# A transformer step with 32 experts on one core: the last expert's rows reach their tokens by one-hot products on TensorE instead of through HBM

## The reference

```python
xn  = rms_norm(h, ffn_norm_g)
g   = argmax(xn @ w_router_group)                  # one of 4 groups
top_v, top_i = top_k(expert logits inside group g, 2)
e_w = softmax(top_v) * softmax(group logits)[g]    # two weights for each token
e_id = g * 8 + top_i                               # two experts for each token
for each expert e, for the tokens that chose it:
    hb = silu(xb @ w_exp_gate[e]) * (xb @ w_exp_up[e])
    y  = hb @ w_exp_down[e]
out[token] = h[token] + sum over its two experts of e_w * y
y   = rms_norm(out, final_norm_g)
```

## Time and profile before

| what | value |
|---|---|
| median of 3 runs | 1102.0 us (1099.07 to 1102.05) |
| profiled execution's own time | 1100.63 us |
| its span in the trace | 1099.1 us |
| PE busy | 943.1 us, 86% |
| DVE busy | 340.9 us, 31% |
| ACT, POOL busy | 202.2 us and 197.9 us, 18% each |
| HBM read and written | 267.41 MB and 23.17 MB |

### The profile page before, as it was taken

The page is one execution under the profiler, slowest core; times in us unless marked ns, Lnnn a source line. Parts: engine busy times, 40 slices in busy tenths (PEclk is TensorE's granted clock), DMA queues, the critical chain, the costliest instruction groups (busy, mean ns, idle before and its releaser), DMA issues.

```text
span 1099.1 us, 12164 instructions
## 1 busy us (share of the span) xinstructions
PE 943.1 (86%) x4705; PEld 532.2 (48%) x4705; DVE 340.9 (31%) x756; ACT 202.2 (18%) x446; POOL 197.9 (18%) x296
## 2 busy tenths in 40 slices
PE   7978999999999998999994999888778887878870
PEld 6634444767776656774552434434334242442420
DVE  2269999973441111331226000100000000000016
ACT  3243110213343424000220110000000000000012
POOL 2730660100001110000132111111111111111122
PEclk9989999999999999999996999999999999999995
DMA  9920212512202545933027999999999999999985
GB/s 337 392 86 1 77 47 76 183 53 77 77 1 89 218 154 164 335 149 153 19 96 283 413 421 422 421 423 425 423 422 425 422 425 421 424 425 424 419 320 188
DMA packets 53402, 283.82 MB, mean 258 GB/s; under 512 B 8652, under 2 KB 9520, under 8 KB 32999
## 3 DMA queue, kind: packets, MB, share of 16 engines
q1 hardware_dynamic: 42519, 246.24, 55.8%
q0 software_dynamic: 10784, 36.97, 9.3%
q10 hardware_dynamic: 56, 0.01, 0.0%
HBM read 267.41 MB, written 23.17 MB: 264 GB/s over the span
## 4 chain that ended last, share of the span: by engine, by line
PE 47%; DMA 29%; DVE 18%; ACT 2%; issue 2%; SPq 1%; POOL 0%; ACTq 0%; POOLq 0%; DVEq 0%; PEldq 0%
DMA arena<-in_w_exp_up 24%; PE psum L798 9%; DVE arena L1442 6%; DVE arena L1440 6%; PE psum L952 5%; PE psum L1038 5%; PE psum L934 4%; PE psum L1035 4%; PE psum L1036 3%; PE psum L1053 3%; DMA arena<-in_w_branch_pool 3%; PE psum L622 3%; PE psum L886 1%; DMA y_d<-arena 1%; PE psum L634 1%
## 5 line engine op out<-in xcount | busy, mean ns | idle before, releaser
L1038 PE MATMUL psum<-arena 128*64 128x512 f32 x704 | 169.1, 636 | 30.5 <-DMA arena<-in_w_exp_up 29.8
L1053 PE MATMUL psum<-arena 128*64 128x512 f32 x512 | 116.9, 597 | 17.7 <-ACT arena L1335 17.7
L798 PE MATMUL psum<-arena 128*128 128x288 f32 x480 | 126.1, 416 | 0.0
L1038 PEld LDWEIGHTS psum<-arena 128*64 128x64 f32 x704 | 55.7, 146 | 142.1 <-issue 108.1
L798 PEld LDWEIGHTS psum<-arena 128*128 128x128 f32 x480 | 89.6, 192 | 31.0 <-issue 8.1
L1679 DVE TENSOR_TENSOR arena<-arena,psum 128x256 f32<-128x256 f32 x32 | 13.5, 421 | 277.3 <-ACT arena L1331 277.3
L608 PE MATMUL psum<-arena 128*128 128x512 f32 x192 | 86.2, 604 | 2.1 <-ACT arena L1202 2.1
L1331 ACT ACTIVATE arena<-psum 128x256 f32<-128x256 f32 x32 | 12.3, 383 | 405.1 <-PE psum L1038 277.1
L1053 PEld LDWEIGHTS psum<-arena 128*64 128x64 f32 x512 | 40.4, 136 | 72.1 <-issue 71.4
L1687 DVE COPY arena<-psum 128x512 f32<-128x512 f32 x31 | 21.4, 691 | 152.2 <-PE psum L1053 152.2
L1440 DVE MAX8 arena<-arena 64x8 f32<-64x1032 f32 (+3 forms) x80 | 66.2, 828 | 2.8
(11 more groups left out here) (279 smaller groups left out, 1021.4 us busy)
## 6 DMA issues: line engine op xcount, KB each, us to landing
arena<-in_w_exp_down SPq DMA_DIRECT2D x32, 2048.0 KB, 37.0
arena<-in_w_exp_gate SPq DMA_DIRECT2D x30, 2048.0 KB, 32.7
arena<-in_w_exp_up SPq DMA_DIRECT2D x20, 2048.0 KB, 37.2
arena<-in_w_exp_up SPq DMA_DIRECT2D x24, 1024.0 KB, 34.6
arena<-in_w_in SPq DMA_DIRECT2D x7, 2048.0 KB, 8.7
y_d<-arena SPq DMA_DIRECT2D x1, 8192.0 KB
arena<-in_x_prompt SPq DMA_DIRECT2D x8, 512.0 KB, 7.0
arena<-in_w_out SPq DMA_DIRECT2D x2, 2048.0 KB, 10.9
```

The costliest lines, as they stand in the source:

```text
L798: last = pe.matmul(bank(2 + n % 2 if n < SAMPLE_G else 2, HN), ring[slot % 2][:, k, m * P:(m + 1) * P], xnT[:, k, HN * hh:HN * hh + HN], s ...
L1038: last = pe.matmul(bank(2 + s, 512, rows).rearrange("p (w n) -> p w n", w=2), x_k, wgu[j][:, :, DE * k + 256 * q:DE * k + 256 * q + 256], ...
L1053: last = pe.matmul(bank(4 + s, 512, slice(64 * half, 64 * half + 64)), hT[s][:, k % 2, CAP * (k // 2):CAP * (k // 2) + CAP], wd[j][:, k, 5 ...
```

## The change

Expert 31 is no longer written to HBM. Its 64 result rows stay in `yo[1]`, as two halves of 512 columns on partitions 0 to 63 and 64 to 127.

- During routing, DVE builds `lasthot`, for each token a row of 64 numbers: its weight at the place of its rank in expert 31, zero elsewhere (14 small instructions in place of 3, and 2 wide ones of 640 columns). New weights split the cases: `w_high` is `w_hi` for higher slots that are not of expert 31, `w_last` the weight of a slot that is.
- After the second expert, PE turns `lasthot` (5 transposes into banks 6 and 7), and ACT copies it to `lastT`.
- After expert 31, PE multiplies `lastT` with `yo[1]`: two matmuls for each tile (one for each 512 columns), into two banks; tile 4 uses banks 0 and 1 again, after DVE has taken tile 0 from them. PE reads `over` and jumps before that.
- POOL drops the scatter of expert 31 and the wait for its landing; it gathers the higher slots right after its own jump, now from `y_d[0:FIRST - CAP]`, with slots of expert 31 out of bounds.
- DVE has, for each tile, one more instruction in the tail: an add of the product from PSUM into `resid`, ahead of the add of the gathered higher rows. ACT writes its squares to SBUF, not PSUM, since PSUM is in use.
- Some buffers in SBUF move closer together.

```diff
 # DVE, at the end of the routing
-            link(dve.tensor_tensor(gw, s1, s2, ALU.min))
-            link(dve.scalar_tensor_tensor(w_early, gw, FIRST - CAP - 0.5, w_lo, ALU.is_lt, ALU.mult))
-            link(dve.tensor_tensor(w_late, w_lo, w_early, ALU.subtract))
+            dve.tensor_tensor(gw, s1, s2, ALU.min)
+            link(dve.tensor_tensor(gmax, s1, s2, ALU.max))
+            dve.scalar_tensor_tensor(w_early, gw, FIRST - CAP - 0.5, w_lo, ALU.is_lt, ALU.mult)
...
+            link(dve.tensor_tensor(w_last, w_last, top1, ALU.add))
+            wide = [P, TILES, 2, CAP]
+            link(dve.tensor_tensor(lasthot, iota[:, 0:CAP].unsqueeze(1).unsqueeze(1).to_broadcast(wide),
+                                   q_last.unsqueeze(2).unsqueeze(3).to_broadcast(wide), ALU.is_equal))
+            dve.tensor_tensor(lasthot, lasthot, w_last.unsqueeze(2).unsqueeze(3).to_broadcast(wide), ALU.mult).then_inc(S["oh_ready"], 1)
 # PE, in the first round of experts
             for c in range(6):
                 expert(0, c)
+                if c == 1:
+                    pe.wait_ge(S["oh_ready"], 2)
+                    for t in range(TILES):
+                        r = rows_of(t)
+                        last = pe.transpose(bank(6 + t // 4, r, at0=(t % 4) * P), lasthot[0:r, t, :, :].rearrange("p h c -> p (h c)"), ident[0:r, 0:r])
+                    last.then_inc(S["x2t"], 1)
 # PE, after the jump
+            def last_rows(t):
+                r = rows_of(t)
+                for half in range(2):
+                    k = slice(CAP * half, CAP * half + CAP)
+                    last = pe.matmul(bank(2 * (t % 4) + half, 512, slice(0, r)), lastT[k, P * t:P * t + r], yo[1][k, :], start=True, stop=True)
+                last.then_inc(S["tile_sum"], 1)
+
+            pe.wait_ge(S["xs2_r"], TILES + 2)
+            for m in M:
+                pe.wait_ge(m["y_ev"], NE // 2)
+            for t in range(4):
+                last_rows(t)
+            pe.wait_ge(S["y_comb"], TILES + 1)
+            last_rows(4)
 # ACT
             expert_pair(0)
+            act.wait_ge(S["x2t"], 2 * TILES + 1)
+            act.copy(lastT[:, 0:SEQ], bank(6)).then_inc(S["xs2_r"], 1)
+            act.copy(lastT[:, SEQ:NT], bank(7, NS)).then_inc(S["xs2_r"], 1)
...
-                act.activation(psum[0:r, b:b + D], resid[0:r, i, :], ACT.Square, accum_out=ss3[0:r, i:i + 1]).then_inc(S["sq3"], 1)
+                act.activation(yg[i][0][0:r, :], resid[0:r, i, :], ACT.Square, accum_out=ss3[0:r, i:i + 1]).then_inc(S["sq3"], 1)
 # DVE, the tail
             for i in range(TILES):
+                r = rows_of(i)
+                dve.wait_ge(S["tile_sum"], i + 1)
+                b = 2 * (i % 4) * 512
+                dve.tensor_tensor(resid[0:r, i, :], psum[0:r, b:b + D], resid[0:r, i, :], ALU.add).then_inc(S["y_comb"], 1)
+                dve.wait_ge(S["y_comb"], TILES + 2 * i + 1)
                 dve.wait_ge(s_y[i], 32)
-                add_rows(i, 1, w_hi).then_inc(S["y_comb"], 1)
+                add_rows(i, 1, w_high).then_inc(S["y_comb"], 1)
                 if i:
                     final(i - 1)
 # POOL, the tail
-            rows_last(0)
-            store_last(0)
-            rows_last(1)
...
-                pool.indirect_dma_start(yg[i][0][0:r, :], None, y_d[0:FIRST - CAP, :], bass.IndirectOffsetOnAxis(ap=dest[0:r, 0, i:i + 1], axis=0),
-                                        bounds_check=FIRST - CAP - 1, oob_is_err=False).then_inc(s_y[i], 16)
-            store_last(1)
+            def early_rows(k):
+                for i in range(TILES):
+                    r = rows_of(i)
+                    if k:
+                        pool.wait_ge(s_y[i], 16)
+                    pool.indirect_dma_start(yg[i][k][0:r, :], None, y_d[0:FIRST - CAP, :], bass.IndirectOffsetOnAxis(ap=dest[0:r, k, i:i + 1], axis=0),
+                                            bounds_check=FIRST - CAP - 1, oob_is_err=False).then_inc(s_y[i], 16)
+
+            early_rows(0)
             pool.wait_ge(S["flag_ready"], 1)
             over = pool.value_load(flag[0:1, 0:1], min_val=0, max_val=NT)
...
-                pool.wait_ge(M[1]["y_st"], 16 * (NE // 2))
-                combine(1, y_d[0:FIRST, :], s_y)
+                early_rows(1)
```

More of the change, by code:

```diff
@@ L296, in program @@
         t32 = [at(o + j * 160, TILES, NE) for j in range(6)]; o += 960
-        gmax, least, top1, top2, vdf, vex, gw, s1, s2, w1, w2, w_lo, w_hi, r1, r2, w_early, w_late = (at(o + j * TILES, TILES) for j in range(17)); o += 17 * TILES
+        gmax, least, top1, top2, vdf, vex, gw, s1, s2, w1, w2, w_lo, w_hi, r1, r2, w_early, w_late, w_high, w_last, q_last = (at(o + j * TILES, TILES) for j in range(20)); o += 20 * TILES
         ghot, gsh, gex = (at(o + j * TILES * EG, TILES, EG) for j in range(3)); o += 3 * TILES * EG
@@ L322, in program @@
         oneb = at(o, 64).bitcast(BF16); o += 64
-        xg = [at(o + s * D, 512) for s in range(2)]; o += 2 * D
+        xg = [at(o + s * 512, 512) for s in range(2)]; o += 1024
         xT = [at(o + s * 512, KD // 2, P) for s in range(2)]; o += 1024
-        sg = [at(o + s * 512, DE // 2) for s in range(2)]; o += 1024
-        hb = [at(o + s * 512, DE // 2) for s in range(2)]; o += 1024
+        sg = [at(o + s * 256, DE // 2) for s in range(2)]; o += 512
+        hb = [at(o + s * 256, DE // 2) for s in range(2)]; o += 512
         hT = [at(o + s * 256, KE // 2, P) for s in range(2)]; o += 512
+        lastT = at(o, NT); o += NT
+        lasthot = at(o, TILES, 2, CAP); o += TILES * P
+        assert o <= SG + 128 + 5632
+        o = SG + 128 + 5632
         yo = [at(W1 - D + s * 512, 512) for s in range(2)]
@@ L1094, in _ @@
                         down(OV, 0, n)
+                pe.wait_ge(OV["y_ev"], N0 + NE * NB)
             with pe.Else():
                 pe.nop()
+            def last_rows(t):
[11 more added lines that the diff above has]
+            last_rows(4)
         @block.scalar
@@ L1671, in _ @@
                 link(dve.tensor_tensor(w, gw, gmax, ALU.add))
-            link(dve.tensor_tensor(gw, s1, s2, ALU.min))
-            link(dve.scalar_tensor_tensor(w_early, gw, FIRST - CAP - 0.5, w_lo, ALU.is_lt, ALU.mult))
-            link(dve.tensor_tensor(w_late, w_lo, w_early, ALU.subtract))
+            dve.tensor_tensor(gw, s1, s2, ALU.min)
+            link(dve.tensor_tensor(gmax, s1, s2, ALU.max))
+            dve.scalar_tensor_tensor(w_early, gw, FIRST - CAP - 0.5, w_lo, ALU.is_lt, ALU.mult)
+            dve.scalar_tensor_tensor(w_late, gw, FIRST - 0.5, w_lo, ALU.is_gt, ALU.mult)
+            dve.scalar_tensor_tensor(top1, gmax, FIRST - CAP - 0.5, w_hi, ALU.is_lt, ALU.mult)
+            dve.scalar_tensor_tensor(top2, gmax, FIRST - 0.5, w_hi, ALU.is_gt, ALU.mult)
+            link(dve.tensor_tensor(q_last, gmax, gw, ALU.subtract))
+            dve.tensor_tensor(w_high, top1, top2, ALU.add)
+            dve.scalar_tensor_tensor(q_last, gmax, FIRST - 0.5, q_last, ALU.is_lt, ALU.mult)
+            link(dve.tensor_tensor(w_last, w_lo, w_early, ALU.subtract))
+            dve.tensor_tensor(w_last, w_last, w_late, ALU.subtract)
+            dve.scalar_tensor_tensor(q_last, q_last, float(CAP - FIRST), gw, ALU.add, ALU.add)
+            link(dve.tensor_tensor(top1, w_hi, w_high, ALU.subtract))
+            link(dve.tensor_tensor(w_last, w_last, top1, ALU.add))
[3 more added lines that the diff above has]
+            dve.tensor_tensor(lasthot, lasthot, w_last.unsqueeze(2).unsqueeze(3).to_broadcast(wide), ALU.mult).then_inc(S["oh_ready"], 1)
             def expert_h(m, s, n):
@@ L1893, in _ @@
                     scatter_y(s, M[s]["y_st"])
[L1894 to L1901, removed]
-            rows_last(0)
-            store_last(0)
-            rows_last(1)
+            pool.wait_ge(M[0]["y_st"], 16 * (NE // 2 - 1))
+            pool.tensor_copy(syid[0], rowy[:, NE - 2:NE - 1]).then_inc(S["sidx_set"], 1)
+            pool.wait_ge(S["sidx_set"], 2 * NE - 3)
+            pool.wait_ge(M[0]["y_ev"], NE // 2)
+            scatter_y(0, M[0]["y_st"])
             pool.wait_ge(S["dest_ready"], 1)
@@ L1926, in _ @@
                 for s in range(2):
-                    pool.wait_ge(M[s]["y_st"], 16 * (NE // 2))
+                    pool.wait_ge(M[s]["y_st"], 16 * (NE // 2 - s))
                     pool.wait_ge(M[s]["y_done"], NE // 2)
@@ L1940, in _ @@
                 for n in range(YZ):
-                    pool.dma_start(beyond[n], zeros).then_inc(S["y_zero"], 16)
-                pool.wait_ge(S["y_zero"], 16 * YZ)
+                    pool.dma_start(beyond[n], zeros).then_inc(S["zero_st"], 16)
+                pool.wait_ge(S["zero_st"], 16 + 16 * YZ)
                 with pool.Fori(0, NE) as e:
```

13 lines of the change are left out of this document (4 added, 9 removed).

## The result

The changed kernel took 1102.32 us (median of 19 runs, 1099.82 to 1106.11), the kernel before 1099.65 (19 runs, 1096.44 to 1102.94). The ratio is 1.0022, 95% interval [1.0013, 1.0031]: about 2.4 us longer, within the 0.3% that I had called no change, and inside the range. The three runs known beforehand had a median of 1102.0, which was high; by the profiled executions the step is 1102.54 - 1100.63 = 1.9 us.

A forecast was written before the change was run, and what follows sets the result against it. Weight loading bounds the expert stage; the tail is bound by a store and gather through HBM, then DVE. DVE's row gives +1.9 us: 1102.5 by the execution, 1103.9 by the median, forecast 1103.2, range 1100.3 to 1106.5.

The forecast's parts named there:

- The adds from PSUM go one for one onto DVE's path: DVE's tail: each of five adds from PSUM costs 1.25 us with nothing overlapping; four more between second adds, 5.0 us.
- the sum: DVE's tail: the last add starts at 1093.29 instead of 1091.40, so the kernel takes 1.9 us longer.
- The start of DVE's row: Tail: after lower adds, reading `over` and the jump, DVE's first add from PSUM starts at 1078.07 (1077.99 to 1078.3).
- the reading of `over` on the path: DVE's tail: reading begins at 1076.9, branch ends at 1077.87; formerly under a 4.09 us wait, now on the path.
- no gain from lower rows landing sooner: Tail: DVE starting up to 1.1 us earlier was not taken; as a rival it gave +0.8 us, 1101.4, chance 0.08.
- Rival 1: DVE's jump in the tail: code fetched late costs 1.7 us, +3.6 in all, more with a busy queue; chance 0.18.
- Rival 2: Tail: the five adds from PSUM cost nothing on the path, so -3.3 us, 1097.3 by the execution; chance 0.06.
- Rival 3: Start of the weight stream: the load at 630.75 has no cover, 1.0 us more, +2.9 in all; chance 0.06.
- the cover: Load behind PE's transposes: loads already issued keep DMA busy to 635, covering 4 us, so the 1.0 us delay costs nothing.
- The longer routing on DVE: Routing: added DVE instructions take 4.0 us, hidden in DVE's 8.46 us wait for the first expert; no cost.
- The 1103.2: Whole kernel: the forecast time in us, taken between 1102.5 by the execution and 1103.9 by the median; forecast chance 0.62.
- the middle: Whole kernel: the value taken between 1102.5 us by the profiled execution and 1103.9 by the median of runs, 1103.2.

The follow-up runs named there:

- experiment 1: The changed kernel without DVE's five adds from PSUM, the last expert's share left out of the result; ratio to the kernel before 0.9964.
- experiment 8: The changed kernel with PE's eight products of tiles 0 to 3 made three times; ratio to the kernel before 1.0023.
- experiment 4: The changed kernel with DVE reading `over` before its five lower adds, the branch left in place; ratio to the kernel before 1.0015.
- experiment 2: The changed kernel with expert 31's scatter and the wait for its landing put back, its rows not read; ratio to the kernel before 1.0037.
- experiment 5: The changed kernel with the PSUM adds placed between the lower adds and PE's products ahead of its branch; ratio to the kernel before 1.0007.
- Experiment 3: The kernel before plus only the longer routing, PE's transposes and ACT's copies, their result unused; ratio to the kernel before 0.9991.
- experiment 6: The changed kernel with PE adding the lower sums in PSUM, DVE's higher add reading PSUM, the five extra adds gone; ratio to the kernel before 0.9980.
- experiment 7: The changed kernel with the sum formed on PE and `over` read before the lower adds; 1095.53 us, ratio to the kernel before 0.9964.

## Why the prediction was right

- *The adds from PSUM go one for one onto DVE's path.* Right, and the term that decides: 1.22 us each in the row, 6.0 us for five by experiment 1 (the sum had put in 1.25 each, with the wait on the one before).
- *The start of DVE's row.* First add from PSUM predicted at 1078.07, found at 1077.95; then 1079.32, 1081.77, 1085.61, 1089.45, 1093.29 against 1079.22, 1081.67, 1085.52, 1089.37, 1093.21. That the places agree to 0.1 us is luck: in experiment 8, with the same row on DVE, the first add from PSUM starts at 1077.14. What is confirmed is the length of the row, from that add to the last higher add: 15.22 us predicted, 15.26 after the change and 15.25 in experiment 8. The parts are confirmed too: the reading of `over` on the path (0.9 us, experiment 4), no gain from lower rows landing sooner (the last lower add starts at 1075.52, before at about 1074.38 + 1.20 = 1075.58).
- *Rival 1, code fetched late.* Did not happen: the branch ends at 1077.74 + 0.07 = 1077.81 and the add starts at 1077.95, 0.14 us later; reading and jump together leave the same 1.16 or 1.17 us of idle time in experiments 1, 2, 5 and 8. The DMA view of the changed kernel lists no packet on its two instruction queues from 1075 to 1085, and three from 1065 to 1075.
- *Rival 2, the gain promised by the chain.* Its condition, that the adds cost nothing on the path, was wrong. Experiment 1 is the kernel without them, and there the gain against before is 4.0 us, near the 3.3 that the rival gave. With the adds in the row, leaving out the scatter that the chain had named (5.97 us) is worth 1.7 us (experiment 2), since DVE has lower adds, reading and jump to do until 1077.95 anyway and five adds more from there.
- *Rival 3, a slipped start.* Experiment 3 found no cost. The load behind the transposes was issued at 631.81 instead of 630.75, the 1.0 us that the prediction had priced, and the cover held: the DMA share from 600 to 640 is 0.99, above the 0.97 that I had drawn as a line, and 1.00 before (windows: length; PE, PEld, DVE, ACT, POOL busy; clock; DMA share; GB/s; first after, then before):

```profile
600.00:640.00 40.00, 37.32 (x207) 18.34 (x205) 4.10 (x7) 4.73 (x11) 5.46 (x10) 1.00 0.99 407
```

```profile
600.00:640.00 40.00, 37.24 (x206) 18.35 (x204) 3.34 (x6) 4.02 (x9) 6.36 (x11) 1.00 1.00 415
```

- *Where a size was off.* I had the higher rows land from 1078.0 to 1087.4, at the pace of the lower ones. They were all there by 1084.1. It didn't matter, as the row of DVE is later still; why they came faster wasn't tried. PE's pair for tile 4 took 1.97 us, at a granted clock of 0.50, within its cover. The longer routing on DVE took some 3.2 us, not 4.0: DVE's wait for the first expert fell from 8.46 to 5.30 us.
- *The time.* The sum of +1.9 us met the execution's own 1.9 and the tail's 2.1; the runs' +2.4 [1.4 to 3.4] holds it. That single executions met it so closely is luck in part: against experiment 3, with the tail of before, the tail's step would be 3.5. The 1103.2 lay 0.9 above the median measured, and there two errors partly cancel: the middle that I took with the high median of three runs put the kernel before at 1101.3, 1.7 too high, and the step between the medians is 2.7, 0.8 more than the sum.

## What to carry to other kernels

Work that is taken off a chain of transfers and given to the engine that finishes the kernel pays only as far as that engine has pauses: here 6.6 us of delay removed were worth 1.7 with the five instructions of 1.2 us in that row, and some 4 without them; the five cost 6 where the engine waited for nothing any more, and some 4 where it still waited for rows. Add up that engine's whole row from its new start to the end before trusting the chain of waits. Where TensorE stands idle beside it and one-hot products go into PSUM anyway, let it form the whole sum there, and let an instruction that the finishing engine has to run anyhow read PSUM: here (experiment 6) 4.6 us less than the changed kernel by the ratio.

## What the runs showed of the hardware

- *Half-size products on different partitions went nearly twice as fast.* In experiment 6 the one-hot products of 64 rows took 3.70 us for 16 records (0.23 each) and the identity's of 128 rows 7.13 (0.45). For tile 4 both are 64 rows by 64 columns: the pair whose halves lie on different partitions (0 to 63 and 64 to 127) took 1.07 us for four records, the pair whose halves both lie on partitions 0 to 63 took 1.93 (experiment 7: 1.08 and 1.93). So it is not the 64 rows alone. The identity's products also add to what is in the bank; that this makes them slower wasn't tested by itself, but the experts' down products, which add up over four steps, take 0.23 a record too (L1053 before, 16 records in 3.65 us). The two comparisons give factors of 1.9 (7.13 against 3.70) and 1.8 (1.93 against 1.07); why is not shown.
- *PE's clock after a rest.* After the change PE had nothing to do for 6.40 us before tile 4's pair, which then ran at a granted clock of 0.50 and took 1.97 us (the same 0.50 and 1.97 us after 8.10, 8.08 and 6.61 us in experiments 1, 2 and 4); in experiment 6 the same pair came right behind other products, at 1.00, and took 1.07. The windows of the two stretches, after the change and in experiment 6:

```profile
1079.20:1081.20 2.00, 1.97 (x4) 0.29 (x4) 1.98 (x2) 0.67 (x1) 0.00 (x0) 0.50 0.43 109
```

```profile
1078.60:1081.60 3.00, 2.93 (x8) 0.62 (x8) 2.54 (x4) 2.73 (x6) 0.00 (x0) 1.00 0.20 59
```

- *Reading a word of SBUF into a register on DVE* took 0.54 us and 0.23 us of register work (L1746 after the change), in all 0.9 us on the path (experiment 4): a cost to place under a wait.
